# Token half 1 five weight chunks behind token half 0, instead of four, with the same ten slots

## What is computed

```python
def swiglu_2(x, w_in, w_out):
    gate, up = jnp.split(x @ w_in, 2, axis=-1)
    return (jax.nn.silu(gate) * up) @ w_out
...
    # first_block: HGRN2 mixer and gMLP mixer, merged, @ w_o, then
    x = x + mod[:, 5, None] * swiglu(h2, w_up[l], w_down[l])
    return rmsnorm(x, g_final)
...
    # second_block, for two layers (stick-breaking attention, then latent attention)
    f = swiglu_2(rms_norm(x, g[0]), ffn_w_in[i, 0], ffn_w_out[i, 0])
    x = x + FFN_RESIDUAL_WEIGHT * rms_norm(f, g[1])
    h = rms_norm(x, g[2])
    x = x + rms_norm(m, g[3])          # m: attention of h
    f = swiglu_2(rms_norm(x, g[4]), ffn_w_in[i, 1], ffn_w_out[i, 1])
    x = x + FFN_RESIDUAL_WEIGHT * rms_norm(f, g[5])
```

## Time and profile before

| what | value |
|---|---|
| median of three runs | 1463.91 us |
| the profiled execution: its own time | 1463.74 us |
| its span, first to last instruction | 1462.5 us |
| TensorE busy | 1433.3 us, 98% of the span |
| VectorE busy | 856.6 us, 59% |
| ScalarE busy | 755.1 us, 52% |
| the core's 16 DMA engines busy, by queue q1 | 52.7% |
| mean granted TensorE clock | 0.997 |

### The profile page before, as it was taken

The page is one execution under the profiler, slowest core; times in us unless marked ns, Lnnn a source line. Parts: engine busy times, 40 slices in busy tenths (PEclk is TensorE's granted clock), DMA queues, the critical chain, the costliest instruction groups (busy, mean ns, idle before and its releaser), DMA issues.

```text
span 1462.5 us, 19657 instructions
## 1 busy us (share of the span) xinstructions
PE 1433.3 (98%) x8098; PEld 1205.4 (82%) x8098; DVE 856.6 (59%) x1191; ACT 755.1 (52%) x1086; POOL 22.9 (2%) x72
## 2 busy tenths in 40 slices
PE   7999999999999999999999999999999999999998
PEld 5999889978888788888897888887888879888886
DVE  4628766875554755556355655557555475755553
ACT  4435355555453655445565655446455476755442
POOL 0000000000000000000121000000000000000000
PEclk9999999999999999999999999999999999999999
DMA  9437666555555555555433555565555552355552
GB/s 382 153 102 300 240 232 215 175 171 185 186 187 189 196 185 185 185 191 192 165 116 123 177 183 183 187 194 188 185 184 187 185 182 73 116 184 186 190 186 89
DMA packets 69930, 267.34 MB, mean 183 GB/s; under 512 B 7760, under 2 KB 8016, under 8 KB 66384
## 3 DMA queue, kind: packets, MB, share of 16 engines
q1 hardware_dynamic: 67680, 259.13, 52.7%
q10 hardware_dynamic: 2160, 6.95, 1.4%
HBM read 265.00 MB, written 1.05 MB: 182 GB/s over the span
## 4 chain that ended last, share of the span: by engine, by line
PE 91%; DVE 5%; ACT 2%; DMA 1%; issue 1%; SPq 0%; POOL 0%; DVEq 0%; ACTq 0%
PE PS L728 24%; PE PS L744 14%; PE PS L746 14%; PE PS L745 14%; PE PS L371 5%; PE PS L373 4%; PE PS L372 4%; PE PS L712 2%; PE PS L403 1%; PE PS L404 1%; PE PS L405 1%; DMA MC<-in_mod 1%; PE PS L472 1%; DVE WL L1652 1%; DVE TN L2099 1%
## 5 line engine op out<-in xcount | busy, mean ns | idle before, releaser
L1652 DVE TENSOR_TENSOR WL<-RAW,WH 128x1024 fp32r<-128x1024 f32 (+1 forms) x440 | 532.0, 1221 | 330.0 <-ACT WH L1093 329.5
L1093 ACT ACTIVATE WH<-RAW 128x1024 fp32r<-128x1024 f32 (+1 forms) x440 | 454.2, 1054 | 299.7 <-DMA RAW<-in_up 178.6
L744 PE MATMUL PS<-WH,XH 128*128 128x512 f32 (+1 forms) x928 | 380.9, 410 | 9.2 <-DVE XL L2107 9.0
L746 PE MATMUL PS<-WH,XL 128*128 128x512 f32 (+1 forms) x928 | 362.1, 390 | 0.0
L745 PE MATMUL PS<-WL,XH 128*128 128x512 f32 (+1 forms) x928 | 361.7, 390 | 0.0
L744 PEld LDWEIGHTS PS<-WH,XH 128*128 128x128 f32 x928 | 174.3, 188 | 59.5 <-DVE XL L2107 13.9
L746 PEld LDWEIGHTS PS<-WH,XL 128*128 128x128 f32 x928 | 174.2, 188 | 37.2
L745 PEld LDWEIGHTS PS<-WL,XH 128*128 128x128 f32 x928 | 175.0, 189 | 27.7
L728 PE MATMUL PS<-WH,GH 128*128 128x512 f32 x440 | 137.3, 393 | 0.0
L728 PE MATMUL PS<-WL,GH 128*128 128x512 f32 x440 | 135.8, 390 | 0.0
L728 PE MATMUL PS<-WH,GL 128*128 128x512 f32 x440 | 135.6, 389 | 0.0
(11 more groups left out here) (344 smaller groups left out, 1821.6 us busy)
## 6 DMA issues: line engine op xcount, KB each, us to landing
RAW<-in_up SPq DMA_DIRECT2D x220, 512.0 KB, 4.7
RAW<-in_down SPq DMA_DIRECT2D x110, 512.0 KB, 3.2
RAW<-in_win SPq DMA_DIRECT2D x44, 512.0 KB, 6.2
RAW<-in_mod SPq DMA_DIRECT2D x16, 1024.0 KB, 6.8
MC<-in_mod SPq DMA_DIRECT2D x8, 1024.0 KB, 13.6
RAW<-in_sbqk SPq DMA_DIRECT2D x16, 512.0 KB, 4.7
GROW<-in_grow ACTq DMA_DIRECT2D x9, 512.0 KB, 4.6
RAW<-in_wo SPq DMA_DIRECT2D x8, 512.0 KB, 4.1
```

The source lines that it names most:

```text
L744: e.matmul(o_[:, 0:n], l, w[:, s], start=(k == 0), stop=False, skip_group_check=True)
L746: m = e.matmul(o_[:, 0:n], ll, w[:, s], start=False, stop=(k == KD - 1), skip_group_check=True)
L1093: e.activation(WH[s][:, 0:c], RAW[s][:, 0:c], ACT.Copy).then_inc(*sig("hi", j))
L1652: e.tensor_tensor(WL[s][:, 0:c], RAW[s][:, 0:c], WH[s][:, 0:c].bitcast(F32), ALU.subtract).then_inc(*sig("lo", j))
```

## The change

`LAG` goes from 4 to 5, with SLOTS = 10 and AHEAD = 3 as they were. In the hand-written order of block 2's output projection, half 1 likewise falls one chunk further behind. ScalarE's and VectorE's gate and split of half 1's gated tiles move one index later in their loops. And the two PSUM banks with half 0's down sums are held from the first down step until half 1's last gated tile has been turned (loop index UP + 3 of half 1), since the ring would otherwise come back to them.

```diff
-LAG = 4
+LAG = 5
...
                         if between:
                             next(between)
+                        if d == 0 and h == 0:
+                            for n in range(2):
+                                BANK.hold(("dn", v, 0, n))
+                        if p == UP + 3 and h:
+                            for n in range(2):
+                                BANK.release(("dn", v, 0, n))
...
                 if pr >= 8:
                     sbo_step(2 * pr - 16, 1)
-                    sbo_step(2 * pr - 15, 1)
+                    if pr == 8:
+                        sbo_step(1, 1)
                     sbo_step(pr - 2, 0)
...
-            for k in range(4, 8):
+            for k in range(3, 8):
                 sbo_step(k, 1)
                 if k >= 6:
                     turn(3, 0, k - 6)
...
                     j, z = p // 4, p % 4
-                    if z == 0 and 3 <= j < FT // 2 + 3:
+                    if z == 1 and 3 <= j < FT // 2 + 3:
                         gated(v, j - 3, 1)
-                    if z == 0 and 2 <= j < FT // 2 + 2:
+                    if z == 1 and 2 <= j < FT // 2 + 2:
                         gate(v, j - 2, 1)
                     split(c0 + p + AHEAD)
...
                     if z == 0 and 1 <= j < FT // 2 + 1:
                         gate(v, j - 1, 0)
-                    if z == 0 and 2 <= j < FT // 2 + 2:
+                    if z == 1 and 2 <= j < FT // 2 + 2:
                         gate(v, j - 2, 1)
                     if z == 1 and 2 <= j < FT // 2 + 2:
                         gated(v, j - 2, 0)
-                    if z == 1 and 3 <= j < FT // 2 + 3:
+                    if z == 2 and 3 <= j < FT // 2 + 3:
                         gated(v, j - 3, 1)
                     split(c0 + p + AHEAD)
```

## The result

The changed kernel takes 1483.27 us (median of four runs, 1482.03 to 1483.78), the kernel before on the same chip 1464.11 us. The ratio is 1.0124, with a 95% interval from 1.0111 to 1.0136: slower by 18 us by the ratio, 19 by the medians. The forecast was slower by 12, and its range ended at 1481. The profiled execution took 1483.78 us, with a span of 1482.5 us.

The account below looks back on a forecast made before the run. TensorE was taken as the bound, busy 98% of the span, so the change could only close or open gaps. New waits summed to 12.1 us on the profiled 1463.74, giving 1475.8 us, with a range of 1467 to 1481.

Parts of the forecast that it names:

- The extra step: At the block heads: closes little, since one step still follows the turning; only waits for X in blocks 0 and 1 go.
- the waits for WL: At the block heads: TensorE would newly wait for the splits' low parts, some 6 us at L744, near each seventh chunk.
- The terms of `wo`, blocks 0, 1, 2 and 4, and of the output projection: Losses in us: `wo` 0.7; heads of blocks 0, 1, 2, 4: 2.0, 2.1, 1.2, 1.0; output projection 0.8.
- the tight chunk: Heads 2, 3, 4, 6: c0 + 7 split later and wanted earlier; new waits of 1.2, 1.4, 1.0 and 1.2 us.
- the waits for X: Heads of blocks 0 and 1: the turning's own waits for late X, 0.38 and 0.36 us, would go.
- which the change leaves as it is: Block 5: its 2.56 us of TensorE's wait for XL stay unchanged; no new loss there.
- the two held banks ... nothing: PSUM ring: its turn passes to banks whose gated tiles were split several pairs earlier; cost nothing.
- a bank wait of at most a step at each block: Rival: held banks make a step wait once per SwiGLU block, 7 us more; chance 0.05 together with starvation.
- A clock that falls: Rival: new gaps at six heads bring back the 1.2 GHz level, 16 us more, near 1491; chance 0.03.
- The steady part: no wait: Middle of blocks: slots freed 2.72 us later; block 4's smallest spare of 5.3 us becomes 2.6, so no wait.
- Before block 4: 0.3: At the boundary before block 4: a new wait of 0.3 us, bounds 0 and 1.2.

Follow-up runs that it names:

- e2: The changed kernel with half 1's turning one step earlier, back behind half 0's fourth step: 1476.20 us.
- e3: The changed kernel with chunk c0 + 7 split within the boundary, and c0 + 5 split before the turned tiles in blocks 0 and 1: 1478.73 us.
- e1: The changed kernel with two more PSUM banks held for a moment, so that block 5's first step takes a free one: 1478.93 us.
- e4: The kernel before, lag 4, with the bank ring moved on by two before block 5: 1470.03 us.
- e7: The kernel before with step (5, 0) ahead of (0, 1) at each head, plus the earlier splits of c0 + 7 and c0 + 5: 1463.47 us.
- e6: The kernel before, lag 4, with half 0's step 5 moved ahead of half 1's step 0 at each head: 1461.72 us.
- e11: e6 with half 0's turning one step earlier at the ends ahead of blocks 2, 4 and 5: 1458.79 us.
- e10: e1 with block 3's angle table work moved later, ScalarE's by three steps and the rest of VectorE's by five: 1477.99 us.
- e12: e1 with X renewed ahead of the split of c0 + 2 and the copy of c0 + 3 at block 0's end: 1477.18 us.
- e5: The changed kernel at lag 5 with e1, e2 and e3 together: 1469.48 us.
- e9: e1 with the projection `wo` and block 2's output projection back at lag 4: 1475.04 us.
- e8: e7 with half 0's turning one step earlier at the ends ahead of blocks 2, 4 and 5: 1460.35 us.

## Why the prediction was right, and where not

**Direction and mechanism: right.** The extra step buys nothing at the heads, since the turning moves with it. In heads 2, 3 and 4 the 0.34 behind the turning stayed, the waits for WL came, one to three in each of the six heads, L702 waits 1.1 before block 1 and L728 0.6 for OL. e2 and e3 show that the turning's place and the place of the splits behind it make these waits. The terms of `wo`, blocks 0, 1, 2 and 4, and of the output projection hold to within 0.3 us each. Without block 5 and the start of the kernel the profiled execution lost 14.0 against 12.1.

**Inside the heads the sums hold better than their parts.** In heads 2, 3, 4 and 6 I called c0 + 7 the tight chunk and did not do the same sum for c0 + 6. By the earlier trace rows it was ready at 1001.86 and by the earlier trace rows used at 1004.41, 2.55 us to spare, less 2.72: minus 0.17. It costs 0.35 us in each of the four heads and takes as much off the wait for c0 + 7, so the total came out. In heads 0 and 1 I let only the waits for X go, 0.38 and 0.36. The waits for XL behind the turning went too, 1.38 and 0.81, under waits for WL that I had left out, the first being for c0 + 5. So the group for WL is 9.1 us and not some 6, that for XL 5.9 and not 9.0, and that the two errors nearly cancel is luck. Head 6 likewise lost 0.39 of its wait for XL (0.73 before, 0.34 after), which I had not counted; its stretch cost 0.79 against 1.2.

**Block 5, "which the change leaves as it is", and "the two held banks ... nothing": wrong, and the same step.** This is the step that put the time beyond the range. I looked at who gets the skipped banks inside a SwiGLU block, and found work finished long before. I did not follow the ring past the end of block 4. There `ktab` takes one bank that other boundaries don't take, and the first step of block 5 falls on a bank whose sums the boundary itself has yet to read. Term sized 0, measured 5.3. With that wait alone taken out (e1) the median is 1478.93, inside the range of 1467 to 1481. The rival that I named, a bank wait of at most a step at each block with 7 us more, had the right object and the wrong places: it comes once, and is three and a half steps long. The order of takes by bank would have shown it ahead of any run, since the hold is a matter of counting.

**"A clock that falls", 0.03: it fell, at one place.** I argued that no new gap would be longer than the 2.56 us that the earlier trace rows show without harm. With the bank wait there was one of 4.69, and the clock fell behind it in all four kernels that have it (the change, e2, e3, e4). By the way from that step to the second turning it cost 1.6 us in the change, 1.4 in e4 and 2.8 in e2 and e3. The wait for XL behind it, 0.8 us shorter in all four, gives a part of the whole delay back. The six places that I priced at 16 us did not come.

**"The steady part: no wait": wrong by one place.** 5.3 less 2.7 is right for block 4's middle, but I read the spare at one block, and block 3 has 4.25 us of ScalarE's stand in it. A minimum over one block isn't the minimum of the kernel. It cost 1.13 us of idle time in this execution and none in e1, and why the two differ is open.

**Before block 4: 0.3, about right.** TensorE waited 0.73 us for XL there instead of 0.36, and 0.60 in e1. That the work of half 0's boundary stands behind later splits there, as it did before block 1, is argued; no run moved them.

**The start of the kernel, 0.75,** is no part of the mechanism. The program is the same up to `wo`. TensorE waits for MC at L472, and behind it the granted clock is low for a while (17 to 25 us: 0.68 before, 0.55 in the change). Both move from one kernel to the next, whatever was edited behind them: e7 waits 2.8 us for MC where e6 waits 1.9, and enters block 0 1.1 us later. In the change the wait is 1.6 us as before, and the low clock is longer.

## What to carry to other kernels

An order that is fixed on every queue moves as a whole: more distance between two halves helps a wait only if what is waited for keeps its place, and here the turning moved along while the splits behind it lost a step on both sides. To cover a wait, exchange two steps around it (e6, e11) rather than lengthen a constant that all stages share. Do the sum of spares for every chunk behind the turning and for every block, not for the one that looks tightest. Where banks or slots are handed out in a ring, one take or skip more changes every later owner: list the owners over all stages, and look for one that is freed only at a boundary.

## What was not expected of the hardware

The granted clock is not a function of the gap alone. Behind gaps of 4.69 us it fell four times in four. Behind head 5's wait for XL of 2.53 to 2.56 us it fell in e1, e10 and e12, and not in the kernel before, e5, e6, e7 or e9, nor behind 2.31 in e8 and e11; behind 2.15 or 2.16 us in head 0 it fell in e9 and not in the change, e1, e10 or e12; behind 1.97 us in head 1 it fell in e3. Each fall shows the level of 1.2 GHz for some 2 to 6 us and then the level of 2.4 again. It need not begin with the first matmul behind the gap: in e1 TensorE goes on at 1201.86 and the slow matmuls begin at 1202.79. The Trainium skill (TensorE: Matmul & The Clock Gate, Part 1) says that the activity is observed in windows that run free of the kernel; the irregular falls agree with that, and no run here tests it. For a forecast it means that gaps of 2 us and more carry a chance of 1.3 us and more on top (1.3 behind head 5 in e1, up to 2.8 behind 4.69), and that two versions of one kernel can differ by that much with the same waits.

A wait also costs more than its idle time shows, by some 0.26 us a time, as the head of block 4 shows above, and one of 0.35 us is not listed at all. Nine waits for WL of 9.1 us in sum stand for some 11.4 (9.1 + 9 x 0.26, an estimate from that head), and the four unlisted ones for 1.4 more.
